# Forty-one unread TensorE products a layer, between the mixer's output projection and the experts

## The reference

```
x = x + gate1 * mixed                      # mixed = ... @ w_out, the output projection
h = _modulate(x, norm2_g, shift2, scale2)  # RMSNorm, scale and shift
aff = softmax(h @ router_w)                # 16 experts
gate, idx = lax.top_k(aff.T, C)            # each expert takes its C best tokens
xe = h[idx]                                # C = 64 of 512 latent, 16 of 128 context
he = silu(xe @ w1) * (xe @ w3)
x = x + gate2 * scatter_add(gate * (he @ w2), idx)
```

## Time and profile before

| | us |
|---|---|
| median of 3 runs | 2005.06 |
| lowest and highest run | 2003.74, 2011.64 |
| the profiled execution's own time | 2010.78 |
| its span | 2008.9 |
| TensorE busy in the span | 1846.0 (92%) |
| VectorE busy | 1544.8 (77%) |
| ScalarE busy | 1156.3 (58%) |
| mean granted TensorE clock, as a share of 2.4 GHz | 0.963 |

### The profile page before, as it was taken

How to read it: one execution, slowest core, us unless ns; L and a number is a source line. 1 busy time by engine, 2 the same in 40 slices (tenths; PEclk the granted TensorE clock), 3 DMA queues, 4 the chain that set the end, 5 groups by cost and what they waited for, 6 DMA issues and landing times.

```text
span 2008.9 us, 27163 instructions
## 1 busy us (share of the span) xinstructions
PE 1846.0 (92%) x9522; PEld 1304.3 (65%) x9522; DVE 1544.8 (77%) x2270; ACT 1156.3 (58%) x1540; POOL 326.2 (16%) x152
## 2 busy tenths in 40 slices
PE   4999999949999999999969999995999999999993
PEld 2776777836666666666657786784566666666662
DVE  4543646579999999999846364667899999999993
ACT  2410256337787877777642114623677777777772
POOL 0100021030212222121012003112122122122210
PEclk9999999969999999999989999996999999999997
DMA  9468201278999999999852721025799999999973
GB/s 342 163 226 321 84 1 31 107 289 332 368 385 379 376 378 383 386 386 377 289 188 87 261 80 79 9 108 231 296 378 370 386 374 386 376 388 380 383 299 128
DMA packets 86219, 542.02 MB, mean 270 GB/s; under 512 B 6880, under 2 KB 9698, under 8 KB 61572
## 3 DMA queue, kind: packets, MB, share of 16 engines
q1 hardware_dynamic: 75556, 504.10, 64.6%
q0 software_dynamic: 10592, 36.97, 6.8%
HBM read 517.19 MB, written 23.86 MB: 269 GB/s over the span
## 4 chain that ended last, share of the span: by engine, by line
PE 87%; DVE 7%; DMA 2%; ACT 2%; issue 1%; POOL 1%; SPq 0%; DVEq 0%; ACTq 0%
PE bank L1098 53%; PE bank L799 10%; PE bank L976 5%; PE bank L692 2%; PE bank L924 2%; PE bank L1115 1%; PE bank L835 1%; PE bank L939 1%; PE bank L909 1%; PE bank L1108 1%; PE bank L1014 1%; PE bank L997 1%; PE bank L1047 1%; DMA x_res<-arena_z,iscat 1%; DVE ring_r L1957 1%
## 5 line engine op out<-in xcount | busy, mean ns | idle before, releaser
L1378 ACT ACTIVATE arena_h_r<-ring 128x1024 fp32r<-128x1024 f32 x480 | 504.6, 1061 | 163.1 <-PE bank L1098 159.7
L1896 DVE TENSOR_TENSOR ring_r<-ring,arena_h_r 128x1024 fp32r<-128x1024 f32 x470 | 557.6, 1218 | 32.4 <-ACT arena_h_r L1378 25.3
L1098 PE MATMUL bank<-arena_h_r,arena_u_r 128*80 128x512 f32 x1280 | 372.8, 398 | 4.6 <-DVE arena_u_r L1916 4.6
L1896 DVE TENSOR_TENSOR ring_r<-ring,arena_u_r 128x1024 fp32r<-128x1024 f32 x282 | 333.8, 1219 | 13.7 <-ACT arena_u_r L1378 7.1
L1378 ACT ACTIVATE arena_u_r<-ring 128x1024 fp32r<-128x1024 f32 x288 | 301.2, 1059 | 61.0 <-PE bank L1098 61.0
L1098 PE MATMUL bank<-ring_r,arena_u_r 128*80 128x512 f32 x1024 | 318.4, 392 | 0.0
L1098 PEld LDWEIGHTS bank<-arena_h_r,arena_u_r 128*80 128x80 f32 x1280 | 188.2, 151 | 101.2 <-DVE arena_u_r L1916 6.2
L1098 PE MATMUL bank<-arena_u_r 128*80 128x512 f32 x768 | 216.9, 391 | 0.0
L1098 PEld LDWEIGHTS bank<-ring_r,arena_u_r 128*80 128x80 f32 x1024 | 151.9, 148 | 84.8 <-issue 0.7
L644 POOL DMA_INDIRECT x_res<-arena_z,iscat x32 | 91.6, 2861 | 643.3 <-DVE arena_z L1942 643.3
L1098 PE MATMUL bank<-arena_h_r,arena_z_r 128*80 128x512 f32 x640 | 181.2, 397 | 3.6 <-DVE arena_z_r L1931 3.6
(11 more groups left out here) (255 smaller groups left out, 2668.5 us busy)
## 6 DMA issues: line engine op xcount, KB each, us to landing
ring<-in_exp_w SPq DMA_DIRECT2D x192, 2048.0 KB, 10.1
ring<-in_ada_w SPq DMA_DIRECT2D x24, 2048.0 KB, 9.0
ring<-in_w_in SPq DMA_DIRECT2D x8, 2048.0 KB, 19.8
ring<-in_w_out SPq DMA_DIRECT2D x2, 4096.0 KB, 13.4
x_res<-arena_z POOLq DMA_DIRECT2D x10, 512.0 KB, 3.8
xn_dram<-arena_u POOLq DMA_DIRECT2D x10, 512.0 KB, 3.0
arena_z<-x_res SPq DMA_DIRECT2D x10, 512.0 KB, 6.1
arena_z<-x_res POOLq DMA_DIRECT2D x5, 512.0 KB, 3.6
```

What stands on the lines that cost most here:

```text
L1098: mm = pe.matmul(bank[out + n][0:CAP, :], xs[:, c, :], w[:, n * 512:(n + 1) * 512], start=(c == 0 and part == 0), stop=(c == KC - 1 and pa ...
L1378: act.activation(high[c], slot[s][:, c, :], ACT.Copy).then_inc(high_ready, 1)
L1896: v.tensor_tensor(slot_r[s][:, c, :], slot[s][:, c, :], high[c], ALU.subtract).then_inc(low_ready, 1)
```

## The change

Four calls of `keep_clock` are put into TensorE's stream, all into bank 1, and one wait is moved up past a call so that bank 1 is no longer being read when it is written. That wait, for the residual of tile 3, was already there.

```
                 w_out_half(4, 1, KC // 2, KC)
+                pe.wait_ge(x1_done, l * NT + 4)
+                keep_clock(18, 1)
                 norm2_T(4)
-                pe.wait_ge(x1_done, l * NT + 4)
+                keep_clock(3, 1)
                 router(4)
+                keep_clock(7, 1)
                 pe.wait_ge(aff_done, l * 2 + 2)
                 pe.transpose(bank[5][0:EXPERTS, 0:P], aff[:, 4, :], ident).then_inc(affT_mm, 1)
 
+                keep_clock(13, 1)
                 hold(pe, top_done, l + 1, const_in)
                 pe.transpose(bank[6][0:CAP, 0:EXPERTS], topf[:, :], ident[0:EXPERTS, 0:EXPERTS])
```

## The result

| | before | after |
|---|---|---|
| median of 6 runs, us | 2007.9 | 2025.24 |
| lowest and highest run | 2003.74, 2012.41 | 2019.25, 2029.13 |
| span of the profiled execution | 2008.9 | 2020.9 |
| mean granted clock | 0.963 | 0.980 |

The ratio is 1.0093, with a 95% interval of 1.0072 to 1.0114: by the ratio 19 us slower, with 14 to 23 in the interval (the two medians are 17.3 apart). The prediction was 1.0083. TensorE runs at a higher clock on average, and the kernel is slower.

The account below looks back on a forecast made before the run. TensorE was taken to set the experts' pace, so their later start counts in full: 8.4 us in each of two layers, 16.8 us on the median of 2005.06, gives 2021.7, stated as 2021.5 us, range 2012 to 2029.

Parts of the forecast that it names:

- TensorE sets the pace of the experts, and a delay reaches the end in full: In the expert stage TensorE is busy for all of 480 us, so a later start moves the end by as much.
- A product is two records, 0.86 us: Each added float32 product is two TensorE records 0.43 us apart at full clock, 0.86 us in all.
- TensorE's own stream becomes the path: From the last output projection to the index transposes TensorE never waits: 38.0 us, each layer's experts 8.4 us late.
- The fuller clock gives nothing back behind the indices: From the gather to the first expert records: 0 taken as gain, with minus 1.8 to plus 1.8 us a layer.
- The sum: Both layers' delays, 2 x 8.4 = 16.8 us, on the profiled 2010.78 us: 2027.6, or 1.0083 times.
- Products that fit: Rival at the four waits: products of at most 0.5 to 0.6 us fit, 3.6 us a layer gained, 1998 us; chance 0.07.
- Absorption: Rival in the expert stage: transfers are the real bound and catch up after a later start, 2005 us; chance 0.04.
- The clock did not sink in the last group: Rival at the last group: the clock sinks to half, thirteen products cost another 11.2 us a layer, 2044 us; chance 0.06.

Follow-up runs that it names:

- e5: The changed kernel with 39 products in place of 13 in the last group: 1.0334 to the kernel before, 2072.68 us against 2004.19.
- e2: The changed kernel with all 41 products kept, each 256 columns of the mask wide instead of 512: 1.0007 to the kernel before.
- e1: The changed kernel with 12, 1, 4, 7 products in place of 18, 3, 7, 13: 0.9986 to the kernel before, 2003.02 us against 2005.94.
- e4: The changed kernel with only the first group, 18 products ahead of the transposes of tile 4: 1.0016 to the kernel before.
- e8: The kernel before with 12, 1, 4, 7 products, and 4 in place of 2 behind the gathered rows: 0.9993 to the kernel before.
- e10: The kernel of e1 measured again, 12, 1, 4, 7 products: 0.9987 to the kernel before.
- e9: The kernel before with 11, 1, 4, 6 products, and 6 and 4 in place of 3 and 2 around the gathered rows: 0.9996.

## Why the prediction was right

- **TensorE sets the pace of the experts, and a delay reaches the end in full.** Right. From first to last `hidden_T` it was 516.46 to 516.49 us in each layer of all thirteen profiles, whether layer 0's stage began at 440 or, in e5, at 480 us; e5 shows that delays pass on whole.
- **A product is two records, 0.86 us.** Right; 0.861 by e5. This step carried the result, and e2 tested it from the other side.
- **TensorE's own stream becomes the path.** Right: 38.08 us against 38.0, a stretch 8.47 us longer against 8.4, no wait left at the four places. VectorE's longest wait was 6.43 us, not 5. The two conversions in front of it were quicker (2.87 us from start to end, 431.94 to 434.81 in layer 0, where it was 3.52 before: the first took 0.58 us and not 1.25). Why is open: POOL was at work beside them in both kernels (428.26 to 437.54 before, 425.45 to 434.78 after).
- **The fuller clock gives nothing back behind the indices.** Right for the gather, whose wait grew from weight loads' 0.92 us to 1.84 and 2.00 of TensorE's own. For the first expert product 0 was taken, with 1.8 us a layer either way; the profile had 0 in layer 0 and 1.6 in layer 1. That the total came out even so is in part luck: 0.95 was lost again at the end and 0.89 between the two stretches.
- **The sum.** 16.8 us predicted, 16.9 in the two stretches of the profile; the times alone say 14 to 23.
- **The rivals.** Products that fit fall by e5 and by the rows; that they would then do no harm is right (e2). Their 3.6 us a layer of gain was too much: e1 has 2.8 us in all; its stretches are only 0.6 and 0.7 us shorter, since the earlier gather takes longer. That step had moved the gather with the indices and left out what else was on the queues. Absorption falls by e5. The clock did not sink in the last group (1.00 over 1381.3 to 1419.4). The argument against that rival was read loosely: the five products are not in a row, since the transposes of the gathered rows lie between the third and the fourth. Nor is the router of the earlier trace rows tile 1's; in the source it is tile 0's, with the same instructions.

"TensorE: Matmul & The Clock Gate" of the Trainium skill counts a 512-column product at about 216 ns in "Back-to-back issue gap". One record of 0.430 us is twice that and a float32 product four times, as the four passes in "FP8 and Floating Point Precision", "TensorE Precision Notes", would have it.

The best version found is e1's, 12, 1, 4, 7: 2.8 us or 0.14% under the kernel before, in two measurements on two chips whose intervals both end just below 1. It beats both kernels, by less than one run differs from the next, and it is not told apart from the kernels that fill more.

## What to carry to other kernels

Work that fills a wait is free only while it is shorter than the wait, so price one unit from the trace's start times (here a float32 product is two records of 0.43 us) and divide before choosing a count. What counts then is the overshoot after the higher clock's savings behind it, as e4 shows, and not the overshoot alone. A gain of a microsecond or two ahead of a transfer can be lost to what the transfer now runs beside. And before two profiles are compared as wholes, set them against each other piece by piece: here one was ahead by 5.2 us through nothing that the change does.

## What the runs showed of the hardware

- TensorE's clock sank in work without any idle time. In the window from 395 to 405 us of the kernel before, TensorE was busy in all of it, and the mean clock was 0.66: 1.00 up to 398 and 0.50 from 399 to 404, behind eight transposes (from 394.35) and the 32 records of two routers with 16 columns. In the same window of the changed kernel it was 1.00, with the same instructions up to 402.88. From the start of those routers to the last projection record the thirteen profiles have three values in their 26 layers: 9.4 us (7 times), 11.0 (10 times) and 12.6 (9 times). So this place alone moves an execution by 0 to 6.4 us by chance. The six profiles of kernels with 22 or 24 products rise with it, from 1995.1 us (none lost, e8) over 1999.6 and 1999.8 (1.6 lost, e10 and e1) to 2005.3 (6.4 lost, e9).
- An idle stretch does not decide the clock by its length alone. Behind 3.24 us (e2) the router ran at half clock in layer 0 (3.60 us) and almost at full in layer 1 of the same execution (2.13 us). Behind 0.71 and 1.41 us (e1) the clock was at half in the group after the router (0.50 from 420 to 422).
- The 16 records of a router, 16 columns each, took 1.71 us at full clock and 3.57 at half. That is 0.107 us a record at full clock, as much as a record of the transposes with 128 columns took (0.87 us for eight).
